# A hybrid decoder step on one core: order of the first norm, of the recurrent layer's tail and of prompt attention's head

## The reference

```python
h = rmsnorm(x, norm_g) @ w_in                       # q, forget, value, gate; rmsnorm = x * rsqrt(mean(x*x) + eps) * g
f = lb + (1 - lb) * sigmoid(fz); k = (1 - lb) * sigmoid(-fz)
S_t = diag(f_t) S_{t-1} + k_t v_t^T;  o_t = S_t^T q_t          # gla_chunked
x = x + (rmsnorm(o, o_g) * silu(gate)) @ w_out      # a_w_out
x = x + swiglu_ffn(x, ...)
k, v = rmsnorm(k, k_g), v;  logf = log_sigmoid(fz + b_f)        # shared_kv
c_all = cumsum(concat(past_logf, logf_new))
s = q k^T / 8 + cq - ck;  o = softmax(mask(s)) v               # fox_attention, prompt and sample group
x = x + o @ b_wo;  x = x + swiglu_ffn(x, ...)
```

## Time and profile before

| What | us |
|---|---|
| median of 3 runs (2005.95 to 2008.08) | 2006.96 |
| profiled execution | 2006.57 |
| span of its instructions | 2004.7 |
| TensorE busy | 1864.1 (93%) |
| VectorE, ScalarE, GpSimd busy | 936.8, 687.8, 571.4 |

### The profile page before, as it was taken

The page is one execution under the profiler, slowest core; times in us unless marked ns, Lnnn a source line. Parts: engine busy times, 40 slices in busy tenths (PEclk is TensorE's granted clock), DMA queues, the critical chain, the costliest instruction groups (busy, mean ns, idle before and its releaser), DMA issues. The chain is left out here.

```text
span 2004.7 us, 39375 instructions
## 1 busy us (share of the span) xinstructions
PE 1864.1 (93%) x16381; PEld 1704.7 (85%) x16381; DVE 936.8 (47%) x1401; ACT 687.8 (34%) x1069; POOL 571.4 (29%) x268
## 2 busy tenths in 40 slices
PE   4999997899999999999988789888888999999998
PEld 4899996899999999999986656555557999999998
DVE  3666766245555501254638754333333455555000
ACT  4455454332222222255426544333323322222121
POOL 1333232133333433233335300000002333333332
PEclk8999998899999999999988899989998999999999
DMA  4233231222222233222244389999992222223322
GB/s 105 75 91 92 79 99 45 70 82 83 85 85 85 84 86 86 65 76 75 69 147 155 93 305 369 392 390 388 388 370 86 85 82 79 84 85 93 82 81 77
DMA packets 289139, 272.93 MB, mean 136 GB/s; under 512 B 20097, under 2 KB 249570, under 8 KB 288322
## 3 DMA queue, kind: packets, MB, share of 16 engines
q1 hardware_dynamic: 288818, 269.37, 41.7%
q0 software_dynamic: 144, 1.05, 0.2%
HBM read 252.11 MB, written 14.08 MB: 133 GB/s over the span
## 5 line engine op out<-in xcount | busy, mean ns | idle before, releaser
L1913 POOL TENSOR_TENSOR a_wl<-a_wraw,a_wh 128x1024 fp32r<-128x1024 f32 (+2 forms) x91 | 233.8, 2569 | 416.1 <-ACT a_wh L1846 416.1
L1913 POOL TENSOR_TENSOR b_wl<-b_wraw,b_wh 128x1024 fp32r<-128x1024 f32 (+1 forms) x66 | 173.3, 2626 | 298.0 <-ACT b_wh L1846 298.0
L1806 PE MATMUL ps<-xh,a_wh 128*128 128x288 f32 x1104 | 238.1, 297 | 0.0
L1806 PE MATMUL ps<-xl,a_wh 128*128 128x288 f32 x1104 | 237.0, 296 | 0.0
L1806 PE MATMUL ps<-xh,a_wl 128*128 128x288 f32 x1104 | 236.7, 296 | 0.0
L1846 ACT ACTIVATE a_wh<-a_wraw 128x1024 fp32r<-128x1024 f32 (+2 forms) x91 | 100.6, 1105 | 338.7 <-PE ps L1806 319.0
L1846 ACT ACTIVATE b_wh<-b_wraw 128x1024 fp32r<-128x1024 f32 (+1 forms) x66 | 74.9, 1135 | 318.7 <-PE ps L1806 318.7
L1806 PEld LDWEIGHTS ps<-xh,a_wh 128*128 128x128 f32 x1104 | 177.1, 187 | 1.1 <-issue 0.2
L1806 PEld LDWEIGHTS ps<-xh,a_wl 128*128 128x128 f32 x1104 | 177.2, 187 | 0.6
L1806 PEld LDWEIGHTS ps<-xl,a_wh 128*128 128x128 f32 x1104 | 177.2, 187 | 0.6
L1931 DVE TENSOR_TENSOR xT<-xT,ps 128x576 f32<-128x576 f32 x32 | 24.2, 755 | 327.0 <-PE ps L1806 327.0
(11 more groups left out here) (323 smaller groups left out, 3876.3 us busy)
## 6 DMA issues: line engine op xcount, KB each, us to landing
sa_kp<-in_cache_k SPq DMA_DIRECT2D x128, 512.0 KB, 9.6
sa_vp<-in_cache_v SPq DMA_DIRECT2D x102, 512.0 KB, 14.4
a_wraw<-in_w_gate_up SPq DMA_DIRECT2D x44, 512.0 KB, 3.8
b_wraw<-in_w_gate_up SPq DMA_DIRECT2D x44, 512.0 KB, 3.8
a_wraw<-in_a_w_in SPq DMA_DIRECT2D x32, 512.0 KB, 4.2
a_wraw<-in_w_down SPq DMA_DIRECT2D x16, 704.0 KB, 4.6
xl_plain<-in_cache_v SPq DMA_DIRECT2D x22, 512.0 KB, 14.5
b_wraw<-in_w_down SPq DMA_DIRECT2D x16, 704.0 KB, 4.7
```

What stands on the lines that cost most here:

```text
L1806: mm = pe.matmul(ps[0:width(n), bank(n) + a, 0:HALF], wt[:, base(n) + t, 0:width(n)], ap[:, first + t, a * HALF:(a + 1) * HALF], start=kin ...
L1913: pool.tensor_tensor(part(wl, n), part(wraw, n), part(wh, n).bitcast(F32), ALU.subtract).then_inc(e["low"], 1)
```

## The change

- **First norm.** Loads 1 and 3 are issued from ScalarE's queue; the norm's weights come as a broadcast tile of 512 KB instead of a column load. VectorE multiplies the rows by them while they still stand as rows, then rounds the first two weight tiles (`first_weights`), then scales; ScalarE rounds straight from PSUM and VectorE subtracts from PSUM. GpSimd's first low half waits for the third scaling.
- **Tail of the recurrent layer.** The last two passes are written out in another order; head 7 uses buffers and PSUM banks of its own (`outs`, `turns`), and seven of the eight tiles of trunk unit 0 (`BEGUN = 7`) are multiplied in this block, in `next_unit`.
- **End of the projections.** The last key tile turns into bank 0; the last store of key rows is issued by ScalarE.
- **Head of prompt attention.** The past's decay lies in other memory, and its spreads have no wait for the stores of rows; the offsets are summed by VectorE, one column at a time, out of the sums' last columns; ScalarE negates two of the four groups. SP issues the triangle first, and `place` falls apart into `decays` and `parts`. Queries are rounded two units earlier, `store_rows` is in round 3, `store_new` and two value pages in round 4, the key pages in rounds 4, 5 and 6 (two, three, three). GpSimd takes two memsets and the copies for the sample group.
- **Sample attention and last trunk.** The head rows are loaded in prompt attention; one tile of output weights instead of two is loaded, a step earlier, and `t1` has `ready=1`.

```diff
+        k = self.k
+        self.load(sp, 0)
+        self.load(sp, 2)
+        sp.dma_start(self.gains, k.w["a_norm"].rearrange("o (f n) -> o f n", f=KD).broadcast_to([P, KD, P])).then_inc(self.gained, 16)
+        self.load(sp, 4)
...
-            act.wait_ge(self.weighed, c + 1)
-            act.activation(k.xh[:, :, cols], self.y[:, c % 3, 0:KD * n].rearrange("p (f n) -> p f n", f=KD), ACT.Copy).then_inc(self.high, 1)
+            act.wait_ge(self.turned, c + 1)
+            act.activation(k.xh[:, :, cols], self.banks(c), ACT.Copy).then_inc(self.high, 1)
...
+    def vector(self, dve, first_weights):
+        k = self.k
+        dve.wait_ge(self.gained, 16)
+        for c in range(5):
+            n, _ = self.tokens(c)
+            dve.wait_ge(self.loaded[c], 16)
+            dve.tensor_tensor(self.scaled[0:n, c], self.rows[c][0:n], self.gains[0:n], ALU.mult).then_inc(self.weighed, 1)
+        first_weights()
         dve.wait_ge(self.rooted, 2)
         for c in (0, 2, 4):
             n, _ = self.tokens(c)
-            dve.tensor_scalar(self.scaled[0:n, c], self.rows[c][0:n], self.mean[0:n, c:c + 1], None, ALU.mult).then_inc(self.even, 1)
-        dve.wait_ge(self.consts, 16 * len(k.first_loads) + 16)
+            dve.wait_ge(self.weighed, c + 1)
+            dve.tensor_scalar(self.scaled[0:n, c], self.scaled[0:n, c], self.mean[0:n, c:c + 1], None, ALU.mult).then_inc(self.even, 1)
         for c in range(5):
-            n, _ = self.tokens(c)
-            dve.wait_ge(self.turned, c + 1)
-            if c >= 3:
-                dve.wait_ge(self.low, c - 2)
-            banks = k.ps[:, 2 * (c % 4):2 * (c % 4) + (1 if c == 4 else 2), :].rearrange("p a (f n) -> p (a f) n", n=n)
-            dve.tensor_tensor(y[:, c % 3, 0:KD * n].rearrange("p (f n) -> p f n", f=KD), banks,
-                              self.gain[:].unsqueeze(2).broadcast_to([P, KD, n]), ALU.mult).then_inc(self.weighed, 1)
-            if c >= 1:
-                low(c - 1)
-        low(4)
+            _, cols = self.tokens(c)
+            dve.wait_ge(self.high, c + 1)
+            dve.tensor_tensor(k.xl[:, :, cols], self.banks(c), k.xh[:, :, cols].bitcast(F32), ALU.subtract).then_inc(self.low, 1)
...
+                def next_unit(first_head, end):
+
+                    n = UNITS * H
+                    for t in range(first_head, end):
+                        pe.wait_ge(e["ylow"], t + 1)
+                        for i, (wt, at) in enumerate(((wh, xh), (wh, xl), (wl, xh))):
+                            for a in range(2):
+                                pe.matmul(ps[:, a, 0:HALF], wt[:, n % 2, t, :], at[:, t, a * HALF:(a + 1) * HALF],
+                                          start=t == 0 and i == 0, stop=False)
...
+                pe.wait_ge(e["evicted"], UNITS * H)
+                for f in range(4):
+                    first.raw_turn(pe, f)
+                scores(H - 1)
+                means(H - 2)
+                states(H - 1)
+                pe.wait_ge(e["attended"], H)
+                for f in (4, 5):
+                    first.raw_turn(pe, f)
+                outputs(H - 1)
+                pe.wait_ge(e["low"], UNITS * H + 1)
+                pe.wait_ge(e["advanced"], H)
+                next_unit(0, 2)
+                means(H - 1)
+                next_unit(2, BEGUN)
+                for f in (6, 7, 8):
+                    first.raw_turn(pe, f)
...
+                for f in range(4):
+                    first.raw_copy(act, f)
+                token_rows(H - 1)
+                head_rstd(H - 2)
+                far_blocks(H - 1)
+                for f in (4, 5):
+                    first.raw_copy(act, f)
+                head_out(H - 1)
+                head_high(H - 2)
+                head_rstd(H - 1)
+                for f in (6, 7):
+                    first.raw_copy(act, f)
+                head_high(H - 1)
...
+                pool.wait_ge(first.even, 3)
...
+                def first_weights():
+                    for n in range(2):
+                        dve.wait_ge(loaded[n], 16)
+                        dve.tensor_copy(wh[:, n], wraw[:, n]).then_inc(e["high"], 1)
...
+                attend(H - 1)
+                carry(H - 1)
+                advance(H - 1)
+                for h in (H - 2, H - 1):
+                    head_gate(h)
+                    head_low(h)
...
+                def decays(j):
                     s = j % 2
-                    if j >= 2:
-                        sp.wait_ge(e["scored"], (j - 1) * U)
+                    if j < 2:
+                        sp.wait_ge(ones[j], 2)
...
-                    if j < 2:
-                        sp.wait_ge(e["ones"], 2 * j + 2)
-                    place(j)
+                    if j >= 2:
+                        sp.wait_ge(e["scored"], (j - 1) * U)
+                    if j > 0:
+                        decays(j)
+                    parts(j)
+                    if j == 0:
+                        decays(j)
                     if j == 1:
                         past.load_new(sp)
-                    if j == 2:
+                    if j == 3:
                         past.store_rows(sp)
-                    if j == 3:
-                        sp.wait_ge(past.stored, 32)
-                        keypages.load_early(sp)
+                    if j == 4:
+                        past.store_new(sp)
                         valuepages.load(sp, 0)
                         valuepages.load(sp, 1)
+                        sp.wait_ge(past.stored, 32)
+                        keypages.load_early(sp, 0, 2)
                     if j == 5:
-                        past.store_new(sp)
+                        keypages.load_early(sp, 2, 5)
+                        sp.dma_start(past.headrow, k.w["c_headrow"]).then_inc(past.headed, 16)
+                    if j == 6:
+                        keypages.load_early(sp, 5, 8)
...
+                        for tile in (qb, kb):
+                            pool.memset(tile[DH:DH + 4, 1].bitcast(F32), 1.0).then_inc(ones[1], 1)
...
-                    if w % U in (2, 4) and 2 <= j < KD:
-                        query_high(j, w % U // 2 - 1)
+                    if w % U in (0, 2) and 2 <= j < KD:
+                        query_high(j, w % U // 2)
...
+            for p in range(4 * g, 4 * g + 4):
+                last = p % 4 * P + P - 1
+                dve.wait_ge(self.offset, p + 1)
+                dve.tensor_tensor(self.off[:, p + 1:p + 2], self.off[:, p:p + 1], self.bank(g)[:, last:last + 1], ALU.subtract).then_inc(self.offset, 1)
+            if g % 2 == 0:
+                dve.scalar_tensor_tensor(self.quarter(self.neg, g).rearrange("p (a n) -> p a n", a=4),
+                                         self.bank(g).rearrange("p (a n) -> p a n", a=4), -1.0,
+                                         self.off[:, 4 * g:4 * g + 4].unsqueeze(2).broadcast_to([P, 4, P]), ALU.mult, ALU.add).then_inc(self.negated, 1)
+
+    def act_negate(self, act):
+        for g in (1, 3):
+            act.wait_ge(self.offset, 4 * g + 5)
+            for p in range(4 * g, 4 * g + 4):
+                ins = act.activation(self.neg[:, p * P:(p + 1) * P], self.bank(g)[:, p % 4 * P:(p % 4 + 1) * P], ACT.Identity, scale=-1.0,
+                                     bias=self.off[:, p:p + 1])
+            ins.then_inc(self.anegated, 1)
...
-                    if n == BLOCKS * NB + 2:
+                    if n == BLOCKS * NB + 1:
                         sp.wait_ge(e["filled"], ring["key", NB - 1, 3 * J - 1] + 1)
-                        next_weights(0)
-                        next_weights(1)
+                        next_weights()
...
+                    for t in range(begun if n == 0 else 0, depth(n)):
...
+    def last_store(self, act):
+        k, e, cols = self.k, self.e, slice(SEQ, D)
+        act.wait_ge(e["keyrows"], KD)
+        act.dma_start(k.out["k_sample"].rearrange("b q h d -> (b q) (h d)")[:, cols], self.krows[0:NS, 4, cols]).then_inc(self.row_stored, 16)
+
+    def key_bank(self, j):
+        return 4 if j < KD - 1 else 0
...
-                trunk(k, "t0", gains, 0, a["a_w_out"][0], heads=heads, ready=2)
+                trunk(k, "t0", gains, 0, a["a_w_out"][0], heads=heads, ready=2, begun=BEGUN)
...
-            trunk(k, "t1", gains, 1, a["b_wo"][0], split=Split(k, oT, k.fh[:, 0:KD, :], k.fh[:, KD:2 * KD, :]), ready=2, small=small)
+            trunk(k, "t1", gains, 1, a["b_wo"][0], split=Split(k, oT, k.fh[:, 0:KD, :], k.fh[:, KD:2 * KD, :]), ready=1, small=small)
```

More of the change, by code:

```diff
@@ L186, in tensor @@
             if c == 4:
[L187 removed]
+                pe.wait_ge(self.low, 1)
             for f in range(KD):
@@ L366, in scores @@
                     if h > 0:
-                        pe.wait_ge(e["logged"], h)
+                        if turns[h] == 6:
+                            pe.wait_ge(e["logged"], h)
+                        else:
+                            pe.wait_ge(first.raw, 4)
                         pe.wait_ge(e["keyrows"], h)
```

(8 more changed lines are left out.)

337 lines of the change are left out of this document (162 added, 175 removed).

## The result

The changed kernel takes 1982.73 us (median of 4 runs, 1982.51 to 1986.14) against 2007.05 for the kernel before on the same chip: ratio 0.9887, 95% interval 0.9874 to 0.9899. The sign was forecast, the size was not: 24 us were gained where I forecast 39, and 1982.73 lies outside the range of 1956 to 1981. The profiled execution has a span of 1980.9, 23.8 less than before.

The account below looks back on a forecast made before the run. TensorE, busy 93% of the span, was taken as the bound; gains come where it waits or runs slow. -6.9 - 11.9 - 9.0 - 11.2 - 1.3 - 4.5 + 5.5 = -39.3 from 2006.57, plus 0.4: 1967.7; range 1956 to 1981.

Parts of the forecast that it names:

- D: Prompt attention: placement waits shrink as queries are rounded earlier and pages spread over rounds; -11.2, or -10.3 with the first exponential inside.
- store_new in round 4 ... I give it 1.0 of stall: Prompt attention: store_new waits for VectorE at pair 4, so placement 5 goes out some 6 us into it; 1.0 stall.
- the 8.83 of pair 4: Prompt attention: TensorE's wait for pair 4's placement behind ten pages, 8.83 us, of which 8.4 was credited as gained.
- +0.9 for the page sums before the first exponential: Head of prompt attention: VectorE's column sums and ScalarE's negations delay the first exponential by 0.9 us, hidden by nothing.
- placements still starve: Rival, chance 0.12: in prompt attention the ten pages are paid in pairs 5 to 7 instead of pair 4, +12.6: 1980.
- E1: Sample attention, start and end, to its last pick: -1.3 and -4.5, together -5.8 us.
- The start's -1.3: Start of sample attention: head rows loaded before, so TensorE's wait of 3.03 shrinks; VectorE's memsets limit this to -1.3 us.
- the -4.5 at the end: End of sample attention: one output-weight load dropped, the other moved earlier, so the last value pages come sooner; -4.5 us.
- E2: Last trunk: ScalarE waits for the second weight tile and rounds it before unit 0's splits; +5.5 us.
- B: Tail of the recurrent layer and first trunk: earlier scores and outputs, seven eighths of unit 0 done early; -11.9 us.
- A: First norm: VectorE weighs rows and rounds weights earlier, first matmul at 27.5 instead of 33.38; -6.9 us.
- C: Projections' end to first scores: earlier block start, spreads without waiting for stores, no offset matmuls; -9.9 us before the +0.9.

Follow-up runs that it names:

- e1: Changed kernel with the store of the new rows' decay issued after the placement of pair 5 instead of in round 4; ratio 0.9863 to the kernel before.
- e2: Changed kernel with two value pages and first two key pages issued after the placement of pair 5, the store left in front; ratio 0.985 to the kernel before.
- e8: Changed kernel with the new rows' running sum moved from VectorE to GpSimd, after its parts of pair 3; ratio 0.9838 to the kernel before.
- e11: Changed kernel with VectorE's memset of ones and query packing in sample attention put behind its first two key copies; ratio 0.9891 to the kernel before.
- e6: Changed kernel without the hold on GpSimd's first two low halves in the first norm; ratio 0.9905 to the kernel before.

## Why the prediction came out as it did

The sum went wrong in D first of all. **"store_new in round 4 ... I give it 1.0 of stall"** is the step that failed: it measured 6.2 in the first profile, 3.2 to 6.2 in nine (mean 4.3). I had named the wait of SP and the four pages, but had the placement issued some 6 us into pair 4 and in time but for that 1.0. In the first profile the pair starts at 1071.87, the store goes out at 1076.42, and the placement is issued from 1082.16 to 1085.2, that is 10.3 to 13.4 into the pair. It lands behind the pages' 2 MB, 7.2 after its last issue. e1 and e2 show that neither the pages nor the store's wait costs anything at pair 5 without the other. The second failure in D is an omission: I crossed out the 8.83 of pair 4 and did not ask what ran under it. VectorE's chain of 3.0 did; e1 shows it as 2.7 of wait and a low clock behind it, and in e8 both are gone. Together these two are the 11.4 between 45.2 and 33.8 (9.6 on the mean of nine). The third is at pair 0: the +0.9 for the page sums before the first exponential was 1.2, but TensorE's pause grew with it, in eight profiles of eleven a low clock followed, and the pair grew by 3.0. The six placement waits themselves went as forecast, 14.2 to the one at pair 5. I had named "where a page round meets a placement" as one of the two places where I would be wrong first, and so it was. The rival "placements still starve" named it too and, at 1980, came nearest to the time. That nearness is luck: it has 12.6 over pairs 5 to 7 where the runs show 3.2 to 6.2 at pair 5 alone, and the other stages made up the rest.

E1: -5.8 forecast, -1.8 in the first profile, -4.1 on the means. The start's -1.3 measured 0.0, by the first page's issue, which comes 6.2 behind the first turn in both: the wait moved from the head rows to VectorE's memset, 2.5 for 3.0. I had seen that memset and credited what was left of the wait; e11 shows another wait behind that one. For the -4.5 at the end, -2.3 showed in the first profile and -3.6 on the means of nine against three (345.3 and 348.9), with ranges that overlap: by the means it is mis-sized by about 1, and the rest can't be told from the spread between executions. Of TensorE's 3.6 at the last pages 2.3 stayed. (Pair 7's own end is the other 0.5.)

E2: +5.5 measured +6.7 to the first matmul. The mechanism was right and ScalarE's part too (5.2, of my 5 to 6). VectorE's first subtraction, held up beside GpSimd for 1.7, is the term that I did not have. The other 0.8 is a low clock that lasts 5.9 us behind the first matmul instead of 4.3.

B: -11.9 forecast, -9.5 in this profile, -5.8 to -14.9 over thirteen, mean -10.4. The scores were ready at 329, as forecast (336.6 less the 7.7 of A). The term that was off is states, 5.8 us at the low level where I put 3.0. It is the execution's, not the code's: in the five profiles where the clock stayed up states took 3.04 and the tail beat my number.

C: -9.9 forecast, -9.0 measured. The first scores came 11.9 after the block's start where I forecast 11.7, for offsetting reasons: the sums took 5.5 instead of 7.0, and waited 2.2 past the last spread for the triangle, a load I had not counted. The rest is the block's start, which came 1.75 sooner after the second addition and not 2.3. A: -6.9 forecast, -7.7 measured (-4.1 to -7.7 in fourteen profiles, median -6.1). In the first profile all 2.8 of the low clock went instead of my 1.9, and the gains cost 1.3 on VectorE instead of 0.9. Over the fourteen, the way from the first matmul to the gate copy takes 287.2 to 290.6, mean 288.7, against 289.8 before: on average only 1.1 of the low clock went, so my 1.9 was too high by 0.8, where the first profile makes it look too low.

## What to carry to other kernels

When a wait goes, list what each other engine did under it: in-order work that was free there comes back at its full price, and here also at half the clock. When a wait is added to a queue, count what gets ahead of the next urgent transfer while it stands, not only the wait. And a load moved nearer to its use should be waited for as late as its first user allows; two exchanged lines brought the first matmul 6.8 us nearer. Last, read a stage from several profiles before its terms are compared with a forecast: here the same code differed by 4 to 9 us in a stage.

## What the runs showed of the hardware

TensorE's clock falls after pauses that look harmless, but not after each: behind 1.82 us at pair 0 it was 0.50 for some 7 us, and 1.00 in three other profiles with the same pause; behind 2.70 it was low for 9 us in e1 and 3 in e2, behind 2.75 for 14, while in the earlier trace rows a pause of 3.03 was followed by full speed. In the recurrent tail the same code fell in eight profiles of thirteen and did not in five, which is worth 4 to 9 us of that stage. At the first matmul of the kernel it was low in nine of fourteen. So neither "it will" nor "it won't" can be forecast from one trace.

VectorE and GpSimd hold each other up although they share no data: three scalings 6.28 instead of 2.07, four packings 3.02 instead of 0.85 (beside a mere memset), one subtraction 2.4 instead of 0.8. VectorE's subtractions of the first norm, with an operand in PSUM, were not stretched: two ran beside GpSimd's halves and took 1.23 each, against 1.21 in e6, where the halves had ended.

A load of 64 KB (the triangle) behind a stage's last stores took 6.4 and 6.7 us to land in the two profiles of the changed kernel, against 3.3 in the kernel before, where it was issued 2.5 us into the block.
